# An encoder block on eight cores: gate and value projections during the arrival of the tokens, other homes for the late weights and z tiles, and a last block in parts

## The reference

```python
xn = _rmsnorm(h, norm_g)
v_c, g_c, z_c, u_s, z_s, gl_c, gl_s = _split_columns(xn @ w_in)
y_c = silu(layernorm(causal_dwconv31(v_c * sigmoid(g_c)))) * silu(z_c)   # 1024 channels
y_s = gelu(s5_scan(u_s))                                                 # 64 groups, 64 complex states
y_s = y_s * sigmoid(y_s @ w_glu + b_glu) * silu(z_s)
merged = sigmoid(gl_c + b1) * (y_c @ w_conv) + sigmoid(gl_s + b2) * (y_s @ w_ssm)
out = _rmsnorm(h + merged @ w_out, final_g)
```

## Time and profile before

| | us |
|---|---|
| median of 3 runs (lowest, highest) | 1707.64 (1706.62, 1712.65) |
| the profiled execution, its own time | 1703.25 |
| its span on the slowest core (core 6) | 1701.6 |
| PE, DVE, ACT, POOL busy on that core | 1623.4, 714.3, 532.5, 117.4 |

### The profile page before, as it was taken

How to read it: one execution, slowest core, us unless ns; L and a number is a source line. 1 busy time by engine, 2 the same in 40 slices (tenths; PEclk the granted TensorE clock), 3 DMA queues, 4 the chain that set the end, 5 groups by cost and what they waited for, 6 DMA issues and landing times.

```text
span 1701.6 us, 25563 instructions; the slowest of 8 cores (1688.3 to 1701.6 us)
## 1 busy us (share of the span) xinstructions
PE 1623.4 (95%) x9402; PEld 917.5 (54%) x9402; DVE 714.3 (42%) x1265; ACT 532.5 (31%) x926; POOL 117.4 (7%) x226
## 2 busy tenths in 40 slices
PE   4789999999999999997999999999999999999997
PEld 3668878888855444443444444444444444444443
DVE  4668346887866343275311112222111111225433
ACT  3346333555465684253011111111111111122221
POOL 1100000000000000000000000000100100100000
PEclk7899999999999999998999999999999999999999
DMA  9982666577676923327544444445565553926612
GB/s 234 183 163 50 121 115 136 125 146 155 125 162 147 237 71 86 86 72 156 107 83 76 75 75 74 75 75 87 87 99 87 90 98 74 202 95 231 214 75 75
DMA packets 115114, 200.85 MB, mean 118 GB/s; under 512 B 19376, under 2 KB 68784, under 8 KB 112816
## 3 DMA queue, kind: packets, MB, share of 16 engines
q0 software_dynamic: 36672, 102.86, 36.8%
q1 hardware_dynamic: 78032, 95.30, 18.5%
q10 hardware_dynamic: 288, 1.06, 0.2%
HBM read 248.92 MB, written 42.53 MB: 171 GB/s over the span
## 4 chain that ended last, share of the span: by engine, by line
PE 85%; DMA 10%; DVE 2%; ACT 1%; issue 1%; SPq 1%; POOL 0%; DVEq 0%; ACTq 0%; POOLq 0%
PE ps L350 85%; DMA CY<-x_t 3%; DMA ST<-z_scr 2%; DMA u_scr<-ST 2%; DVE CY L324 1%; DMA SM<-par 1%; SPq L362 1%; DMA CY<-c_scr 1%; DMA CY<-par_b 1%; ACT ST L317 1%; DMA a_scr<-ST 1%; ACT L317 0%; DVE XM L335 0%; PE ps L619 0%; ACT CY L317 0%
## 5 line engine op out<-in xcount | busy, mean ns | idle before, releaser
L350 PE MATMUL ps<-XM,WS 128*128 128x512 bf16 (+1 forms) x5888 | 1020.7, 331 | 27.5 <-ACT ST L340 13.3
L350 PEld LDWEIGHTS ps<-XM,WS 128*128 128x128 bf16 x5888 | 578.6, 99 | 428.1 <-issue 34.8
L317 ACT ACTIVATE ST<-ps,SM 128x512 f32<-128x512 f32 (+2 forms) x224 | 136.4, 626 | 634.4 <-PE ps L350 628.1
L335 DVE SCALAR_TENSOR_TENSOR ST<-ps,ST 128x512 f32<-128x512 f32 x132 | 91.1, 690 | 513.3 <-PE ps L350 512.4
L350 PE MATMUL ps<-CY,WS 128*128 128x512 bf16 x1280 | 288.9, 381 | 16.0 <-DVE CY L324 16.0
L350 PEld LDWEIGHTS ps<-CY,WS 128*128 128x128 bf16 x1280 | 125.5, 98 | 168.2 <-issue 18.2
L324 DVE TENSOR_TENSOR CY<-CY 128x257 f32<-128x257 f32 (+3 forms) x192 | 126.0, 671 | 53.9 <-ACT CY L317 40.8
L317 ACT ACTIVATE ST<-ps 128x258 f32<-128x258 f32 (+1 forms) x136 | 65.2, 485 | 186.8 <-PE ps L350 184.6
L317 ACT ACTIVATE CY<-CY 128x514 f32<-128x514 f32 (+3 forms) x112 | 96.5, 875 | 69.6 <-DMA CY<-x_t 34.4
L324 DVE TENSOR_TENSOR CY<-ps,CY 128x514 f32<-128x514 f32 (+1 forms) x96 | 65.1, 686 | 79.4 <-PE ps L350 73.9
L362 POOL DMA_DIRECT2D WS<-w_main x102 | 54.2, 531 | 540.0 <-PE ps L350 387.4
(11 more groups left out here) (80 smaller groups left out, 798.8 us busy)
## 6 DMA issues: line engine op xcount, KB each, us to landing
WS<-w_main POOLq DMA_DIRECT2D x102, 512.0 KB, 7.2
WS<-w_br POOLq DMA_DIRECT2D x32, 512.0 KB, 5.1
CY<-x_t POOLq DMA_DIRECT2D x20, 516.0 KB, 23.3
WS<-w_dw POOLq DMA_DIRECT2D x32, 320.0 KB, 7.5
z_scr<-ST SPq DMA_DIRECT2D x64, 128.0 KB, 3.4
ST<-z_scr SPq DMA_DIRECT2D x32, 256.0 KB, 3.8
WS<-x SPq DMA_DIRECT2D x8, 1024.0 KB, 7.4
CY<-x SPq DMA_DIRECT2D x8, 1024.0 KB, 11.7
```

The lines of the kernel that those rows point to most:

```text
L317: f = lambda e: e.activation(out=out_, in_=in_, func=func, bias=bias, scale=scale)
L335: return S.op("dve", lambda e: e.scalar_tensor_tensor(out=out_, in0=in0, scalar=scalar, in1=in1, op0=op0, op1=op1), 0.15 + n / 960.0, read ...
L350: return lambda e: e.matmul(a[0], a[1], a[2], start=a[3], stop=a[4])
```

## The change

**Start.** The wave now projects gate and value of blocks 0 to 3 (`vg_tile`; 32 pairs, 32 stores) with `w_main[8..15]`, the same 1024 matmuls; the state-space inputs follow in the block loop, `u(m + 1)` beside block m, and `vg(m)` from m = 4 on. Two weights that were loaded early into ST (`vg0`) are gone. All token quarters are issued by SP, but for chunk 0's odd ones (ACT), and wait only for their buffers. The weights alone are on POOL. The 90 dummy matmuls at the start become 30 groups of 8 of lowest priority, which the scheduler puts into gaps. The chunk sums get banks 2 to 5 in turn.

**Late weights and z.** The z projection uses slots 0 to 3. The GLU's weights have tiles of their own in the upper half of WS, so that gate weights can be fetched to slots 0 to 3 before the GLU is through; the sixth to eighth gate loads wait for the last multiply by z (`zm`). The z tiles of the GLU get eight buffers, which lie over `mean` and `rstd`.

**Layer norm.** The reciprocal deviation is made by logarithm and exponential on ACT, for the four quarters together, instead of square root on ACT and reciprocal on DVE. The gelus go in pairs and follow the exponentials.

**End.** `o_last` does the sixteenth output block in five parts (512, 512, 512, 256, 256 columns), with a buffer, a sum of squares and a product by `final_g` for each as it comes, and four stores of 256 KB.

```diff
+        PRE_N = 30
...
         def x_load(j):
             for q in range(4):
                 t, b = XQ[j % 3][q]
-                eng = ("act" if q % 2 else "sp") if j == 0 else "sp" if j < 3 else "pool"
+                eng = "act" if j == 0 and q % 2 else "sp"
                 xl[j, q] = dma(eng, [(t, x_t[j][:, q * 4 * NC:(q + 1) * 4 * NC])], f"{eng}x{j % 3}{q}", 128 * 16 * NC, (), (b,),
-                               prio=0 if j == 0 else 1 + j / 10, after=(xl[0, q],) if j == 1 else (xl[0, 3], xl[1, q]) if j == 2 else ())
+                               prio=0 if j == 0 else 1 + j / 10)
...
-            bk = side_bank()
+            bk = 2 + j % 4
...
-
-        S.op("pe", [lambda e: e.matmul(ps[6][:, 0:128], ones_b[:, :], ones_b[:, :], start=True, stop=True)] * 90, 9.0,
-             (CB,), (psB[6],), prio=0)
...
-        uw = []
-        for m in range(8):
-            aft = () if m == 0 else (xl[0, 3],) if m == 1 else (xl[m // 2, 2 * (m % 2)],)
-            uw.append(wload(m, w_main[m], m / 2, after=aft))
...
-        vg0 = []
-        for i in range(2):
-            t, b = tile("ST", o_x + i * 4096, 4096)
-            dma("pool", [(t, w_main[8 + i])], f"vg{i}", 128 * 8192, (), (b,), prio=9, after=(xl[4 + i, 3],))
-            vg0.append((t.rearrange("p (k n) -> p k n", k=16), b))
...
+        for i in range(PRE_N):
+            S.op("pe", [lambda e: e.matmul(ps[7][:, 0:128], ones_b[:, :], ones_b[:, :], start=True, stop=True)] * 8, 0.8,
+                 (CB,), (psB[7],), prio=99, after=(xl[0, 2],))
+
+        vgw = []
+        for i in range(8):
+            aft = () if i == 0 else (xl[0, 1],) if i == 1 else (xl[i // 2, 2 * (i % 2)],)
+            vgw.append(wload(i, w_main[8 + i], i / 2, after=aft)[:2])
...
             s = slot_n[0] % 6
             slot_n[0] += 1
-            return wload(s, w_main[i], prio, after=after)
+            return wload(s, w_main[i], prio, after=() if ahead is None or len(units) < 2 else (units[-2][ahead],))
...
+        def vg_tile(m, j, wg, wgB, wv, wvB, halves=2):
...
+            act(th, ps[bk][:, 0:NC], AF.Tanh, scale=0.5, n=NC, reads=(psB[bk],), writes=(thB,), prio=1)
...
+            o = stt(pt[:, 2:NC + 2], th, 1.0, ps[bk2][:, 0:NC], ALU.add, ALU.mult, n=NC, reads=(thB, psB[bk2]),
+                    writes=(pB,), prio=1)
+            dma("sp", [(a_scr[m][j], pt)], f"pc{pi}", 128 * PCB, (pB,), (ascB[m][j],), prio=5)
...
+            (wg, wgB, _), (wv, wvB, _) = wnext(8 + 2 * m, 30, 2), wnext(9 + 2 * m, 30, 5)
+            units.append([vg_tile(m, j, wg, wgB, wv, wvB) for j in range(8)])
...
+        def u(m):
+            wv, wB, _ = wnext(m, 28, 2)
+            done = []
...
-            dma("sp", [(u_scr[m][j], pt[:, 2:NC + 2])], f"pc{pi}", 128 * NC * 2, (pB,), (uscB[m][j],), prio=5)
...
+        t_m = [16, 26, 35, 44]
+        for _, j, m in sorted((max(t_j[j] + 6, t_m[m]), j, m) for j in range(8) for m in range(4)):
+            vg_tile(m, j, *vgw[2 * m], *vgw[2 * m + 1], halves=4 if j < 2 else 2)
...
+        u(0)
         s5_mats(0)
-        vg(0)
         for m in range(8):
             if m + 1 < 8:
                 s5_mats(m + 1)
-                vg(m + 1)
+                u(m + 1)
+            if m > 3:
+                vg(m)
             conv(m)
             s5_block(m)
...
-            wv, wB, _ = wnext(24 + mm, 31)
+            wv, wB, _ = wload(mm % 4, w_main[24 + mm], 31)
...
             (mt, mB), (rt_, rB) = mean[n], rstd[n]
...
-            stt(rt_, ps[b2_], 1.0 / E, rt_, ALU.mult, ALU.subtract, reads=(psB[b2_], rB), writes=(rB,), prio=PL)
-            act(rt_, rt_, AF.Sqrt, bias=LN_EPS, reads=(rB,), writes=(rB,), prio=PL)
-            recip(rt_, rt_, 64, (rB,), (rB,), prio=PL)
+            var = stt(rt_, ps[b2_], 1.0 / E, rt_, ALU.mult, ALU.subtract, reads=(psB[b2_], rB), writes=(rB,), prio=PL)
+            lnv.append(var)
+        for n in range(4):
+            act(rstd[n][0], rstd[n][0], AF.Ln, bias=LN_EPS, reads=(rstd[n][1],), writes=(rstd[n][1],), prio=PL - 1, after=lnv)
+        for n in range(4):
+            lne = act(rstd[n][0], rstd[n][0], AF.Exp, scale=-0.5, reads=(rstd[n][1],), writes=(rstd[n][1],), prio=PL - 1)
...
+        zr += [tile("ST", 6144 + i * 2048, 2048) for i in range(8)]
+
         def z_load(mm, h, prio):
-            i = zr_n[0] % 3
+            i = zr_n[0] % 3 if mm > 7 else 3 + mm
...
-            act(YS_t[m][0], YS_t[m][0], AF.Gelu_apprx_tanh, n=2048, reads=(YS_t[m][1],), writes=(YS_t[m][1],), prio=16)
+        for m in range(0, 8, 2):
+            S.op("act", [lambda e, a=YS_t[i][0]: e.activation(out=a, in_=a, func=AF.Gelu_apprx_tanh) for i in (m, m + 1)], 3.9,
+                 (YS_t[m][1], YS_t[m + 1][1]), (YS_t[m][1], YS_t[m + 1][1]), prio=14.5, tab="gelu", after=(lne,))
...
-        wg = [wload(i, w_glu[i], 32, n=1024, k=8) for i in range(8)]
+        wg = []
+        for i in range(8):
+            t, b = tile("WS", 16384 + i * 2048, 2048)
+            dma("pool", [(t, w_glu[i])], f"wg{i}", 128 * 4096, (), (b,), prio=32)
+            wg.append((t.rearrange("p (k n) -> p k n", k=8), b))
...
-                    tt(ys, ys, z_, ALU.mult, n=1024, rate=1.92, reads=(YSq[m][n - 1], YSq[m][n], zB), writes=(YSq[m][n - 1], YSq[m][n]), prio=4)
+                    zm = tt(ys, ys, z_, ALU.mult, n=1024, rate=1.92, reads=(YSq[m][n - 1], YSq[m][n], zB), writes=(YSq[m][n - 1], YSq[m][n]), prio=4)
...
-            return wload(s_, src_ap, 33)
+            return wload(s_, src_ap, 33, after=(zm,) if 6 <= g_slot[0] <= 8 else ())
...
+        def o_last(i):
...
+            parts = [(0, 0, 512), (1, 0, 512), (2, 0, 512), (3, 0, 256), (3, 256, 512)]
+            bs, sbs = [Buf() for _ in parts], [Buf() for _ in parts]
+            pre, preB = smt(4)
+            for p, (n, lo, hi) in enumerate(parts):
...
+                tt(vp, ps[bk][:, 0:w], vp, ALU.add, n=w, reads=(psB[bk], b_), writes=(bs[p],), prio=3)
+                jt, jB = jk[p % 2]
+                act(jt[:, 0:w], vp, AF.Square, accum=s_[:, p:p + 1], n=w, reads=(bs[p],), writes=(jB, sbs[p]), prio=3)
+                if p < 3:
+                    tt(vp, vp, fg4[:, n, :], ALU.mult, reads=(bs[p], fgB), writes=(bs[p],), prio=4)
...
+            act(s_[:, 6:7], s_[:, 4:5], AF.Sqrt, bias=pre[:, 2:3], scale=1.0 / D, n=1, reads=(sbs[4], preB), writes=(sB,),
+                prio=3)
+            recip(s_[:, 7:8], s_[:, 6:7], 1, (sB,), (sB,), prio=3)
...
+                stt(vp, vp, s_[:, 7:8], fg4[:, n, lo:hi], ALU.mult, ALU.mult, n=hi - lo, reads=(bs[p], sB, fgB), writes=(bs[p],),
+                    prio=3)
+            for n, eng in ((0, "act"), (1, "act"), (2, "dve")):
+                vp = v_[:, n, :]
+                if eng == "act":
+                    act(vp, vp, AF.Copy, scale=s_[:, 7:8], reads=(bs[n], sB), writes=(bs[n],), prio=3)
...
+                    ts(vp, vp, s_[:, 7:8], None, ALU.mult, reads=(bs[n], sB), writes=(bs[n],), prio=4)
+            dma("sp", [(dst[:, 3, :], v_[:, 3, :])], "hl3", 128 * 2048, (bs[3], bs[4]), (), prio=5)
+            for n, eng in ((0, "act"), (2, "sp"), (1, "act")):
+                dma(eng, [(dst[:, n, :], v_[:, n, :])], f"hl{n}", 128 * 2048, (bs[n],), (), prio=5)
...
-        for i in range(FIRST, 16):
+        for i in range(FIRST, 15):
...
+        o_last(15)
```

More of the change, by code:

```diff
@@ new lines, in u @@
+                pi, pt, pB = chunk_piece()
+                done.append(cp("act", pt[:, 2:NC + 2], ps[bk][:, 0:NC], n=NC, reads=(psB[bk],), writes=(pB,), prio=1))
+                dma("sp", [(u_scr[m][j], pt[:, 2:NC + 2])], f"pc{pi}", 128 * NC * 2, (pB,), (uscB[m][j],), prio=5)
+            units.append(done)
+        t_j = [12 + 9 * j for j in range(8)]
+        t_m = [16, 26, 35, 44]
+        for _, j, m in sorted((max(t_j[j] + 6, t_m[m]), j, m) for j in range(8) for m in range(4)):
+            vg_tile(m, j, *vgw[2 * m], *vgw[2 * m + 1], halves=4 if j < 2 else 2)
@@ L951, in build @@
         PL = 15
+        lnv = []
         for n in range(4):
```

68 lines of the change are left out of this document (39 added, 29 removed).

## The result

The changed kernel takes 1719.94 us (median of 4 runs, 1717.34 to 1723.94) against 1707.64: 1.0068 of before, 95% interval 1.004 to 1.0097. It is slower by 0.7%, where 1665 us was forecast. The profiled execution took 1723.94 us, its slowest core (core 7) 1722.4; PE is busy for 1639.5 us of it (1623.4 before) and idle for 82.9 (78.2 before); of the busy time, dummy matmuls take 19.5 us, and took 7.8 before.

A forecast was written before the change was run, and what follows sets the result against it. Transfers were taken to bound the first 118 us, PE 230 to 568. Gains 18.9 + 2.8 + 16.8 + 3 + 3 - 2 = 42.5 off 1703.25 gave 1660.7, plus 4.4 to the median: 1665 us, range 1648 to 1681.

The forecast's parts named there:

- the step that failed: Blocks: projections and state-space inputs moved into the loop find PE saturated, so moving them costs 0.
- New waits: Gate loads, exponentials and state-space inputs' stores that wait in the new order: a loss of 0 to 4 us, taken as 2.
- Rival D: Start: chunks run in a ring, each paying a 7.8 us wait, norms 22.8 us apart; 1718 us, chance 0.05.
- The start: Arrival up to the first state-space matrices: transfers relieved, DVE comes last; gain 18.9 us, bounds 27 and -6.
- the 20 us for SP's cheaper queue: Arrival: twenty token quarters moved from POOL to SP cost 57 instead of 88 engine-us a MB, saving 20 us of transfers.
- Rival B: Arrival: the queues are alike and transfers bind until 112 us; start gains 11, 1673 us, chance 0.08.
- The interval of 15 us between norms: Arrival: chunk norms follow each other every 15 us, so that the last one ends near 135.5 us.
- The 2.8 for a_scr: First convolution: gate and value stored long before it; 2.8 of the 3.8 us wait gained, bounds 0 to 3.8.
- The gated unit: GLU: PE's 16.0 us wait for a multiply by z shrinks to 1, the clock returns 1.8; gain 16.8 us.
- Rival C: Gated unit: the z tiles gain nothing, as loads come too late or are crowded out; 1682 us, chance 0.10.
- Layer norm and tail: Layer norm: more projections cover the c_scr wait, gain 3 us (0 to 4); tail: last block in parts, 3 (2 to 4.5).
- Rival A: Start: ACT's table changes bound it, each costing another 1.3 us; start loses 8, 1692 us, chance 0.13.

The follow-up runs named there:

- e14: The changed kernel with its order planned at 200 GB/s instead of 320; 0.9924 of before.
- e17: The changed kernel with tokens on POOL as before and its order planned at 200 GB/s; 1.0 of before.
- e18: The changed kernel with its order planned at 150 GB/s instead of 320; 1.0151 of before.
- e6: The changed kernel with the state-space inputs' stores issued by ACT instead of SP; 1713.64 us, 1.0042 of before.
- e9: The changed kernel with two early weights in ST again, for the inputs of blocks 0 and 1; no ratio, typical core's span 5 us above before.
- e15: The changed kernel with tokens issued as before, on POOL from chunk 3 on, chunks 1 and 2 chained; 1.0082 of before.
- e1: The kernel before up to the end of the block loop, with the change's late parts from the z projection on; 0.9921 of before.

## Why the prediction was wrong

**The blocks: the step that failed.** "Its projections, and the state-space inputs moved to the loop, are the same matmuls; they find PE saturated [...] so moving them changes no sum there." The sum is the same, the waits are not: 28.5 us more idle PE on the median core, and a clock of 0.91 to 0.93 where it was 0.97 to 1.00. PE was full in the blocks before because, as I read it, an order had been found in which the loads landed ahead of their use; full engines in a trace show that the covers fit in that order, not that there is room in another. The term "New waits" (0 to 4, taken as 2) took its bound from one a_scr wait that the old order had left; on the slowest core the new waits for L341, u_scr and w_dw alone are 15.3 + 9.5 + 7.1 = 31.9 us. That the order sets the loss in the blocks is shown by e14, e17 and e18, which change nothing but the plan: the same work stands idle for 33.8, 14.5 or 4.9 us there. It is not all of it, since at 200 GB/s the kernel before loses 0.8, and at 150 idle time turns up in other stretches. Which operations matter most stays open: e6 and e14 both fill 230 to 340 us, in e9 one wait takes another's place, and e6 and e9 don't add.

Rival D had 1718 us, close to the measured time, but for a loss of 34 us at the start that did not come; that its number fits is luck.

**The start.** Forecast 18.9, got 3.8 between the two rows (1000 wave matmuls and the matrices done at 177.8 before, at 173.09 + 0.9 = 174.0 after), and about 2 on the median core, since core 6 was a late one. Three terms were off.

The transfers: the 20 us for SP's cheaper queue are not there; on SP the first matrices even stood 9 us later (e15). 88 and 57 engine-us a MB came from different moments, beside other transfers. That transfers cease to bind came true, from about 60 us on instead of 92, but by luck: it was the new wave that relieved them, not the queue (DMA shares above). Whether the number of stores does it or another part of the wave was not separated. The rule of the Trainium skill that the rows seemed to contradict ("Trainium Kernel Development and Optimization", Key Constraints: transfers of all three issuers share the same engines) held: from 30 to 60 us these are full, with a share of 1.01, whether SP brings the tokens (the changed kernel) or POOL (e15). Rival B, at a chance of 0.08, had the queues alike, but also transfers that bind until 112, which did not come.

The interval of 15 us between norms: 16.7 over all, but the first two took 23.1 and 21.7, near rival D's 22.8. In the first, ACT stood 13.57 us for the third chunk's tokens, though the prediction had tokens "there from about 16 us"; the second chunk's logarithm (45.59) and exponential (48.52) stand behind that square, with a tanh (48.24) between them:

```profile
40.56 1.06 ACT L317 ACTIVATE CY<-CY 128x1032 f32<-128x1032 f32 x1 [13.57 <-DMA CY<-x_t]
...
45.59 0.39 ACT L317 ACTIVATE ST<-ps 128x258 f32<-128x258 f32 x1
...
48.24 0.39 ACT L317 ACTIVATE ST<-ps 128x258 f32<-128x258 f32 x1
48.52 0.41 ACT L317 ACTIVATE ST<-ST 128x258 f32<-128x258 f32 x1
```

Then, in DVE's timeline of the changed kernel:

```profile
49.85 6.45 DVE L335 SCALAR_TENSOR_TENSOR XM<-CY,SM,ST 128x258 bf16<-128x258 f32 x16
...
64.65 3.27 DVE L335 SCALAR_TENSOR_TENSOR XM<-CY,SM,ST 128x258 bf16<-128x258 f32 x8
71.74 0.42 DVE L335 SCALAR_TENSOR_TENSOR ST<-ST,ps 128x258 bf16<-128x258 f32 x1 [3.82 <-ACT ST L317]
72.08 2.07 DVE L335 SCALAR_TENSOR_TENSOR XM<-CY,SM,ST 128x258 bf16<-128x258 f32 x5
76.41 0.42 DVE L335 SCALAR_TENSOR_TENSOR ST<-ST,ps 128x258 bf16<-128x258 f32 x1 [2.27 <-PE ps L350]
76.75 1.28 DVE L335 SCALAR_TENSOR_TENSOR XM<-CY,SM,ST 128x258 bf16<-128x258 f32 x3
```

A chunk's norm is cut by multiplies that wait for tanh, which waits behind a square for tokens, or for PE. That is D's ring; it loosened after three chunks, as I read it because PE had a store of work by then. The last norm ends at 150.1, not 135.5.

PE: with chunks that late it had 700 of the 1000 matmuls left at 93 us and ran them to 173 with a single wait of 0.7 us. The prediction had "128 us for 113 of matmuls" for it, and DVE to come last; PE starved until the fourth chunk, and its own matmuls came last.

The 2.8 for a_scr: the wait is gone, but at the same convolution PE now waits 2.5 and 3.6 us for w_dw. The terms given for the range of 1648 to 1681 lead to 1665 - 8 = 1657 and 1665 + 10 + 2 = 1677; the measured time lies outside either range.

**The gated unit: right.** No wait is left in the kernels with eight z tiles (0 us idle in 700 to 860, 14.5 before), but for e18, whose plan brings another one there. Rival C is out.

**Layer norm and tail: right in size.** The c_scr wait is 0.76 us against 3.9. From the end of the last matmul, 1705.62 + 7.11 = 1712.73, to the span's end are 9.7 us instead of 11.8: 2.1, at the low bound of 2 to 4.5. What I missed of the late parts is that they, too, bring a new order to what stands ahead of them (e1: 9.3 us idle between 460 and 700, 4.4 before).

**Rival A: out.** Table loads on ACT in the first 150 us (busy us, mean ns, then idle before):

```profile
L317 ACT ACT_TABLE_LOAD x18 | 23.1, 1283 | 5.6 <-PE ps L620 2.7 <-POOL ST L501 2.1 <-PE ps L350 0.5
```

18, not 30: the prediction gave the exponential another table than tanh, but at 48.52 us it follows a tanh without a load, so of the norms' two only the logarithm takes turns with tanh, and several tanhs lie side by side. And no drain is to be seen:

```profile
41.64 1.28 ACT L317 ACT_TABLE_LOAD   x1
42.94 0.39 ACT L317 ACTIVATE ST<-ps 128x258 f32<-128x258 f32 x1
```
